# Moving the store of the transposed memory tokens behind the twelve weight loads of the memory blocks

## What is computed

```python
def memory_kv(mem, w_kv):
    B, M, _ = mem.shape
    kv = (mem @ w_kv).reshape(B, M, 2, X_HEADS, X_HEAD_DIM)
    return kv[:, :, 0], kv[:, :, 1]
...
    pkv = [memory_kv(mem_prompt, xattn_w_kv[l]) for l in range(DEPTH)]
    mem_k_prompt = jnp.stack([kv[0] for kv in pkv])
    mem_v_prompt = jnp.stack([kv[1] for kv in pkv])
```

## Time and profile before

| | |
|---|---|
| median of 3 runs | 1405.01 us (1404.9 to 1406.42) |
| the profiled execution | 1404.8 us |
| its span, first to last instruction | 1403.0 us |
| PE busy in it | 1350.0 us, 96% |
| DVE busy | 1024.0 us, 73% |
| ACT busy | 756.5 us, 54% |
| POOL busy | 134.4 us, 10% |
| granted TensorE clock, mean | 0.993 of full |
| moved by DMA | 353.67 MB, 252 GB/s in the mean |

### The profile page before, as it was taken

One profiled execution on the slowest core, in us unless ns is written; L12 is line 12 of the kernel. 1 busy time (PEld: TensorE's weight loads), 2 busy tenths in 40 slices (PEclk: granted clock), 3 DMA queues, 4 the chain that ended last, 5 costly groups with the idle time before them and its releaser, 6 DMA issues.

```text
span 1403.0 us, 19745 instructions
## 1 busy us (share of the span) xinstructions
PE 1350.0 (96%) x7689; PEld 1121.5 (80%) x7689; DVE 1024.0 (73%) x1102; ACT 756.5 (54%) x775; POOL 134.4 (10%) x209
## 2 busy tenths in 40 slices
PE   7999999999898999999999999999899999999996
PEld 5888997789676888888887799779777788888884
DVE  3546857782568989898987356783658889898986
ACT  3435633433425876767676353332444777676765
POOL 5000236200000000000000014200000000000000
PEclk9999999999999999999999999999999999999998
DMA  9664464435964999999994455435984799999981
GB/s 321 205 235 151 150 195 116 126 128 229 368 251 158 346 354 348 347 347 355 340 369 129 150 176 188 132 118 170 374 322 165 255 367 343 349 341 343 358 323 38
DMA packets 102002, 353.67 MB, mean 252 GB/s; under 512 B 6368, under 2 KB 32496, under 8 KB 72224
## 3 DMA queue, kind: packets, MB, share of 16 engines
q1 hardware_dynamic: 97056, 336.09, 66.2%
q0 software_dynamic: 4864, 16.45, 3.4%
HBM read 332.85 MB, written 19.67 MB: 251 GB/s over the span
## 4 chain that ended last, share of the span: by engine, by line
PE 80%; DVE 10%; ACT 4%; DMA 4%; issue 1%; SPq 0%; POOL 0%; DVEq 0%; ACTq 0%; POOLq 0%
PE ps L1882 65%; DMA att_kt<-in_cache_mem_v 2%; DMA raw<-in_xattn_w_kv 1%; PE ps L2252 1%; PE ps L2462 1%; PE ps L2275 1%; DVE mix_s L1593 1%; PE ps L1891 1%; PE ps L2263 1%; DVE x L1313 1%; PE ps L1890 1%; DVE x L1310 1%; PE ps L1992 1%; DVE x L1276 1%; DVE stats L1289 1%
## 5 line engine op out<-in xcount | busy, mean ns | idle before, releaser
L1246 DVE TENSOR_TENSOR w_lo<-raw,w_hi 128x2048 fp32r<-128x2048 f32 x64 | 146.1, 2293 | 135.7 <-ACT w_hi L826 135.5
L1882 PE MATMUL ps<-w_hi,xt_hi 128*128 128x512 f32 x576 | 230.0, 399 | 6.0 <-DVE w_lo L1250 2.3
L1882 PE MATMUL ps<-w_hi,xt_lo 128*128 128x512 f32 x576 | 226.0, 392 | 0.0
L826 ACT ACTIVATE w_hi<-raw 128x2048 fp32r<-128x2048 f32 x64 | 121.8, 1912 | 151.0 <-PE ps L1882 91.5
L1882 PE MATMUL ps<-w_lo,xt_hi 128*128 128x512 f32 x512 | 200.9, 392 | 0.0
L1250 DVE TENSOR_TENSOR moe_lo<-moe_in_raw,w_hi 128x2048 fp32r<-128x2048 f32 x72 | 164.2, 2290 | 22.6 <-ACT w_hi L833 22.6
L1250 DVE TENSOR_TENSOR w_lo<-raw,w_hi 128x2048 fp32r<-128x2048 f32 x72 | 164.8, 2292 | 16.6 <-ACT w_hi L833 16.1
L833 ACT ACTIVATE w_hi<-moe_in_raw 128x2048 fp32r<-128x2048 f32 x72 | 138.1, 1918 | 56.4 <-PE ps L1882 56.4
L833 ACT ACTIVATE w_hi<-raw 128x2048 fp32r<-128x2048 f32 x72 | 137.5, 1912 | 14.8 <-PE ps L1882 14.8
L1882 PE MATMUL ps<-xt_hi,w_hi 128*128 128x320 f32 x448 | 138.6, 309 | 0.2
L1882 PE MATMUL ps<-xt_hi,w_lo 128*128 128x320 f32 x448 | 138.4, 309 | 0.0
(11 more groups left out here) (407 smaller groups left out, 2573.1 us busy)
## 6 DMA issues: line engine op xcount, KB each, us to landing
raw<-in_moe_w_gate SPq DMA_DIRECT2D x48, 1024.0 KB, 5.0
moe_in_raw<-in_moe_w_down SPq DMA_DIRECT2D x48, 1024.0 KB, 4.9
moe_in_raw<-in_moe_w_up SPq DMA_DIRECT2D x32, 1024.0 KB, 5.1
raw<-in_moe_w_up SPq DMA_DIRECT2D x32, 1024.0 KB, 5.6
raw<-in_hgrn_w_in SPq DMA_DIRECT2D x16, 1024.0 KB, 5.5
raw<-in_cache_mem_k SPq DMA_DIRECT2D x16, 1024.0 KB, 6.3
moe_in_raw<-in_moe_w_gate SPq DMA_DIRECT2D x16, 1024.0 KB, 5.2
raw<-in_moe_w_down SPq DMA_DIRECT2D x16, 1024.0 KB, 4.9
```

Of the source, the lines that this page charges most:

```text
L826: nc.scalar.activation(hi_at(hi_slot(k)), raw_at(r), ACT.Copy).then_inc(w_high, 1)
L1246: nc.vector.tensor_tensor(lo_at(slot_of(k)), raw_at(slot_of(k)), hi_at(hi_slot(k)).bitcast(F32), ALU.subtract).then_inc(w_low, 1)
L1882: ins = mm(out, lhs, rhs, start=start and n == 0, stop=stop and n == 2, skip_group_check=shared)
```

## The change

The two waits-and-stores keep their form. They stand behind the loads of chunks 3 to 11, which move ahead of them, and the loop over the layers goes on from chunk 12 where it went on from chunk 3.

```diff
             sp.dma_start(x[0:64, 2, :], a["x_sample"].rearrange("b t c -> (b t) c")).then_inc(x_in, 16)
+            groups = None
+            dense(3, 2 * KV_BLOCKS[0], None)
             sp.wait_ge(xt_l, 8)
             for part in range(2):
                 sp.dma_start(mem_rows_kept[part], st_kv[("mem_hi", "mem_lo")[part]][:].bitcast(F32)).then_inc(mem_in[part], 16)
-            groups = None
-            done = 3
+            done = 2 * KV_BLOCKS[0]
             for l in range(LAYERS):
```

## The result

| | before | changed |
|---|---|---|
| median of 5 runs | 1405.01 us | 1397.96 us |
| the five runs | 1404.84 to 1406.42 | 1395.86 to 1399.97 |
| the profiled execution | 1404.8 us | 1396.09 us |
| its span | 1403.0 us | 1394.3 us |

The ratio is 0.9945, with a 95% interval of 0.9931 to 0.996: faster by 0.4 to 0.7%. By the ratio that is some 7.7 us, by the medians 7.05, and by the profiled executions 8.7. The changed kernel's five runs lie 4.1 us apart, those of before 1.6, but that isn't a greater scatter: the kernel before was run again beside the experiments, in groups of 17, 11 and 9, and lies 5.0, 3.9 and 4.3 us apart there (42 runs in all, 1402.16 to 1407.54, median 1405.2).

A forecast was written before the change was run, and what follows sets the result against it. PE, busy 96% of the span, was held by chunk 3's late load; 6.15 us of standing still plus 2.46 us of slow clock, 8.6 us, off 1404.8 gives 1396.2, stated as 1396.3 us, range 1394.8 to 1399.8.

The forecast's parts named there:

- The gap and its price: PE before and during chunk 3: 6.15 us standing still plus 2.46 us of slow clock, 8.6 us to be won.
- the first rival: POOL's small loads share the engines, chunk 3 lands at 25.1 us, PE stops 0.9 us; 1397.2 us, chance 0.13.
- When chunk 3 lands: SP's queue: chunk 3 takes the high store's place and lands at 22.3 us; it has to land by 24.2.
- A landing past 24.2: Sign that the prediction is wrong: chunk 3 landing later than 24.2 us, the time needed for both losses to go.
- The clock term: PE's products of chunk 3 run slowly after the gap; 2.46 us of the gain, 1.2 to 2.9 if slow counts vary.
- What is late next: Chunks 4 and 5 and POOL's constants arrive in time, chunk 4 landing at 26.1 us; everything after moves up 8.6 us.
- What the moved stores meet: SP's queue behind chunk 11: stores land by 70.8 us, chunk 12 at 73.7; ACT idles about 4 us, PE loses nothing.
- the slower rival: Chunk 12 lands behind the moved stores at 82.6 us, costing 5.4 + 2.5 us: 1404.2 us; slower given chance 0.02.
- the waits there and at L1415: ACT at L998 and DVE at L1415 need both stores landed; ACT gets there 14 us after 70.8, costing nothing.

The follow-up runs named there:

- again: The changed kernel run a second time with no edit; median 1396.46 us, ratio 0.9941.
- after_b: The changed kernel run a third time with no edit, on another chip; median 1397.58 us, ratio 0.9944.
- kvout_early: The changed kernel with POOL issuing the store of block 0's `kv_out` between its masks, not behind all its constants; median 1395.81 us.
- store_c3: The changed kernel with the two moved stores right behind chunk 3, ahead of chunk 4, instead of behind chunk 11; median 1399.47 us, ratio 0.9962.
- small_late_c7: The changed kernel with POOL's ten small loads behind its masks and the moved stores behind chunk 7; median 1397.37 us.
- tiny: The changed kernel with the two moved stores cut to an eighth, later load rereading that eighth; 1404.09 us, not comparable.
- tiny_before: The kernel before, stores in their old place but cut to an eighth; end not comparable, last memory block starts at 71.05 us.
- small_late: The changed kernel with POOL's ten small loads of constants issued behind its masks; median 1394.85 us, ratio 0.9926.

## Why the prediction was right or wrong

**The gap and its price** held. 6.15 us of standing still and 2.46 us of slow clock became 0.2 and 0; the last block starts 7.9 us sooner, and the trace ends 8.7 us sooner against a forecast of 8.6. Of the 8.6, chunk 3 and chunk 7 took back 0.2 each, and 0.2 went at the start of chunks 0 and 1, which leaves 8.0, within 0.1 of the 7.9; the other 0.8 us of the 8.7 lie behind the memory blocks, within that part's own scatter. That the trace came so near the forecast is thus in part luck. The median is 1.7 us above the forecast, 1397.96 against 1396.3, and inside the range, but nearer to the 1397.2 of the first rival: executions like again and after_b are as usual as the first.

**When chunk 3 lands** is the step that failed in size: forecast 22.3, deadline 24.2, measured 24.6, 24.8 and 25.6 in the three traces of the changed kernel. A landing past 24.2 stood among the signs that the prediction was wrong, and all three traces show it. I let it inherit the high store's time because it inherited its place and its bytes. It didn't inherit its pace. Part of that is POOL's small loads, the rival to which I had given 0.13: with them moved it landed at 23.05 to 23.5 us in four traces, against 24.6 to 25.6, so they cost some 1 to 2.5 us here. The rest, about 0.8 us against 23.05, fits the slow stretch at 18 to 20 us, but no run shows that. The rival named 25.1 us as the latest end and a loss of 0.9; after_b has 25.6 and 1.0, and kvout_early 26.1. So forecast and rival were two ends of one thing, and executions fall between them and beyond. That the total came right all the same is because PE wanted chunk 3 only at 24.2: it lost 0.2, 0.5 and 1.0 us, not the 2.3 to 3.3 by which the landing was late.

**The clock term.** The 2.46 us went with the gap: the clock stays at 1.00. What a gap costs by the clock varies more than its length does. Slow matmuls behind a gap numbered twelve after 6.15 us, about nine after 3.0 (store_c3), eight after 2.4 (kvout_early), and none at all after 2.8 (small_late_c7, where the granted clock stayed at 1.00). The Trainium skill (TensorE: Matmul & The Clock Gate, Part 1) warns that the number of slow matmuls at a kernel's start differs from run to run of one kernel. No run here repeats one gap, so that isn't shown for gaps; these numbers agree with it in that they don't follow the length. One trace of one gap doesn't give its price.

**What is late next** held for chunk 4, just, and by luck: forecast 26.1 or at worst 30.1, it landed at 30.61, beyond both, and was ready at 34.9 for a PE that wanted it at 35.1. It failed in the sentence that what POOL makes waits for nothing that moves and has room: POOL does wait, by DVE's splits, and its stores of `kv_out` are what ACT needs for chunk 7. That is the mechanism I hadn't named, at 0.2 to 0.9 us in the changed kernel's three traces.

**What the moved stores meet**: the waits stand where they were forecast, the sizes were low. Chunk 11 was said to be untouched, being ahead of the stores; it took 8.8 us to land, not 5.5, and 5.5 in tiny. Chunk 12 came at 76.9 us, not 73.7, against a deadline that had moved to about 78. PE took it up at 82.31 us where the pace would have been 82.17: 0.14 us, all that the slower rival ever cost. The second store landed at 74.3 us, not 70.8, still well before ACT was through with the step ahead of L998, at 86.1; the waits there and at L1415 cost nothing.

## What to carry to other kernels

How late a transfer lands is found first from the bytes ahead of it on its queue, and a transfer that can wait belongs behind those whose consumers can't; tiny_before and store_c3 show it from both sides. When a stall is taken away, look up every engine that used the stall's quiet, here POOL, whose work got slower by 6 us, and every buffer whose release goes through that engine. And when a forecast puts three arrivals within 1 us of their deadlines, forecast a spread, not a time: compare several traces before explaining the median with one, and look how far apart the runs of the kernel before lie before explaining a spread.

## What the hardware showed that I had not expected

- A copy or select on POOL of 0.2 to 0.4 us takes up to 2.3 us when it begins during a DVE subtraction of 2.29 us, and ends with it: once in the kernel before (32.46 to 34.59 us against DVE's 32.25 to 34.54), four times in the changed one. Operations that only write (MEMSET, IOTA) kept their 0.14 to 0.20 us beside such a subtraction in small_late.
- A load of 1 MB issued just ahead of 2 MB of stores landed in 8.8, 6.5 and 7.8 us in the three traces of the changed kernel, and in 5.5 with those stores cut to 256 KB: it wasn't sheltered by its place on the same queue.
- With POOL's small loads (under 0.2 MB) in flight, chunk 4 landed 4.5 to 6.3 us behind chunk 3, without them 2.6. The Trainium skill (DMA: Bandwidth & Descriptors, Queues, rings and completion order) has the engines take packets from the queues in turn; that agrees with these two numbers, and with the kernel before, whose larger packets of the stores moved 391, 402 and 353 GB/s in 18 to 24 us, where chunk 3's packets of 2 KB moved 199, 334 and 268. What slows 18 to 20 us is open: it is at 182 to 257 GB/s wherever chunk 3's load follows `x_sample`, with small loads or without, and at 391 where the store does.
- After gaps of 2.4 and 3.0 us the granted clock fell to 0.50 (kvout_early, store_c3), after one of 2.8 it stayed at 1.00 (small_late_c7).
